# The masks of a diagonal block as the first products of their score banks, in a stick-breaking attention

## The reference, cut to what matters

```
def block(qb, qpb):
    z = jnp.einsum('bqhd,bkhd->bhqk', qb.astype(f32), kf) * (B_DH ** -0.5)
    valid = k_pos[None, :] < qpb[:, None]
    log_keep = jnp.where(valid, jax.nn.log_sigmoid(-z), 0.0)
    after = lax.cumsum(log_keep, axis=3, reverse=True) - log_keep
    a = jnp.where(valid, jnp.exp(jax.nn.log_sigmoid(z) + after), 0.0)
    return jnp.einsum('bhqk,bkhd->bqhd', a, vf)
```

## Time and profile before

| | us |
|---|---|
| three runs, median | 2052.14 (2051.48 to 2052.67) |
| the profiled execution, its own time | 2052.41 |
| its span in the trace | 2050.3 |
| TensorE busy in the span | 1908.9 |
| VectorE busy | 1126.9 |
| ScalarE busy | 1069.3 |

### The profile page before, as it was taken

How to read it: one execution, slowest core, us unless ns; L and a number is a source line. 1 busy time by engine, 2 the same in 40 slices (tenths; PEclk the granted TensorE clock), 3 DMA queues, 4 the chain that set the end, 5 groups by cost and what they waited for, 6 DMA issues and landing times. The chain is left out here.

```text
span 2050.3 us, 35228 instructions
## 1 busy us (share of the span) xinstructions
PE 1908.9 (93%) x11429; PEld 1634.9 (80%) x11429; DVE 1126.9 (55%) x2269; ACT 1069.3 (52%) x2556; POOL 387.1 (19%) x597
## 2 busy tenths in 40 slices
PE   4999999999999899986899999999999999989996
PEld 4888878878878699985777777777777777689995
DVE  5547456465564622554275757575657575754455
ACT  5455455454564521453375657575757575732335
POOL 0133132221331000453010101010101011100341
PEclk9999999999999999998999999999999999999999
DMA  4121121112211252212010101010101010233213
GB/s 152 57 63 36 46 60 56 50 47 57 62 36 47 96 141 66 64 65 73 21 58 27 57 26 57 26 57 26 57 26 57 26 57 26 96 111 97 62 44 131
DMA packets 161746, 124.18 MB, mean 61 GB/s; under 512 B 10992, under 2 KB 152624, under 8 KB 161648
## 3 DMA queue, kind: packets, MB, share of 16 engines
q1 hardware_dynamic: 160784, 122.85, 19.7%
q10 hardware_dynamic: 864, 0.20, 0.0%
HBM read 89.49 MB, written 33.52 MB: 60 GB/s over the span
## 5 line engine op out<-in xcount | busy, mean ns | idle before, releaser
L107 PE MATMUL pj<-area,h_high 128*128 128x384 f32 (+1 forms) x2304 | 666.6, 352 | 26.7 <-DVE lb_qk_low L1360 6.5
L107 PEld LDWEIGHTS pj<-area,h_high 128*128 128x128 f32 (+1 forms) x2304 | 413.6, 184 | 49.1 <-DVE lb_qk_low L1360 7.9
L107 PE MATMUL pj<-area,h_low 128*128 128x384 f32 (+1 forms) x1152 | 394.0, 342 | 0.0
L107 PEld LDWEIGHTS pj<-area,h_low 128*128 128x128 f32 (+1 forms) x1152 | 213.1, 185 | 8.7
L1532 POOL TENSOR_TENSOR lb_o<-lb_o,lb_keep 128x512 f32<-128x512 f32 (+3 forms) x80 | 77.1, 964 | 630.8 <-ACT lb_keep L1232 624.2
L1377 DVE SCALAR_TENSOR_TENSOR lb_s<-lb_sc,lb_m 128x512 f32<-128x512 f32 (+4 forms) x200 | 110.0, 550 | 85.1 <-ACT lb_m L1213 85.1
L1203 ACT ACTIVATE lb_m<-lb_sc 128x512 f32<-128x512 f32 (+4 forms) x200 | 89.1, 488 | 103.9 <-PE lb_sc L1614 41.5
L456 ACT ACTIVATE la_p<-la_sc,la_nm 128x128 f32<-128x128 f32 (+5 forms) x144 | 105.7, 737 | 33.7 <-DVE la_nm L653 32.8
L1408 DVE CAST lb_s_high<-lb_s 128x512 fp32r<-128x512 f32 (+1 forms) x192 | 109.0, 568 | 25.1
L1410 DVE TENSOR_TENSOR lb_s_low<-lb_s,lb_s_high 128x512 fp32r<-128x512 f32 (+1 forms) x192 | 114.6, 597 | 6.6
L651 DVE TENSOR_REDUCE la_mx<-la_sc 128x1 f32<-128x128 f32 (+5 forms) x144 | 107.6, 747 | 2.9
(11 more groups left out here) (307 smaller groups left out, 4470.1 us busy)
## 6 DMA issues: line engine op xcount, KB each, us to landing
stage<-in_a_w_in SPq DMA_DIRECT2D x60, 192.0 KB, 3.0
stage<-in_b_w_in SPq DMA_DIRECT2D x60, 192.0 KB, 2.6
stage<-in_ple_w_gate SPq DMA_DIRECT2D x22, 512.0 KB, 3.9
h_low<-o_t SPq DMA_DIRECT2D x14, 528.0 KB, 6.5
mix_b_xs<-x_mid SPq DMA_DIRECT2D x8, 528.0 KB
lift_xt<-in_x SPq DMA_DIRECT2D x8, 512.0 KB, 4.7
stage<-in_a_w_in SPq DMA_DIRECT2D x16, 256.0 KB, 5.2
out_ak<-la_tok SPq DMA_DIRECT2D x8, 512.0 KB, 3.3
```

What stands on the lines that cost most here:

```text
L107: last = pe.matmul(out, x, y, start=start and n == 0, stop=stop and n == 2, **kw)
```

## The change

On a diagonal pair the two masks no longer follow the score products; they come ahead of them and open the banks (`start=True`), and all score products of the pair add onto them (`start=False` for the first as well). They are a function of their own, `mask(i)`, which is called at the end of turn i - 1, behind the projection, and for pair 0 at the head of turn 0. It waits for the same count of `a` as `scores(i)`. The semaphore `z` is now raised by each head's third score product. The numbers of instructions, their shapes and the sample's pair stay as they are.

```
-                    q = span(c, b)[0]
+                    q, _, diagonal = span(c, b)
                     high, low = qk
                     for n, (x, y) in enumerate(((high, high), (low, high), (high, low))):
                         for s in units(i):
                             f = slice(UNITS[s][2] * DH, (UNITS[s][2] + 1) * DH)
                             last = pe.matmul(bank(s)[:, q:], x[f, 1, b * P:(b + 1) * P],
-                                             y[f, 0, c * QC + q:(c + 1) * QC], start=n == 0, stop=n == 2,
-                                             skip_group_check=True)
-                            if n == 2 and not span(c, b)[2]:
+                                             y[f, 0, c * QC + q:(c + 1) * QC], start=n == 0 and not diagonal,
+                                             stop=n == 2, skip_group_check=True)
+                            if n == 2:
                                 last.then_inc(S["z"], 1)
-                    if span(c, b)[2]:
-                        for s in units(i):
-                            pe.matmul(views(s)[0][:, 0:P], unit[:, :], hide[:, :], **masked).then_inc(S["z"], 1)
+
+                def mask(i):
+                    if not span(*PAIRS[i][0:2])[2] or PAIRS[i][0] == 2:
+                        return
+                    if i >= 2:
+                        pe.wait_ge(S["a"], at.nth("a", through(i - 2)))
+                    else:
+                        pe.wait_ge(S["a"], at.before("a"))
+                    for s in units(i):
+                        pe.matmul(views(s)[0][:, 0:P], unit[:, :], hide[:, :], start=True, stop=False,
+                                  skip_group_check=True)
...
                 for i in range(NP + 1):
+                    if i == 0:
+                        mask(0)
                     if i < NP:
                         scores(i)
...
+                    if i + 1 < NP:
+                        mask(i + 1)
                 values(NP - 1)
```

## The result

Five runs of the changed kernel took 2038.57 us in the median (2033.89 to 2045.80), five of the kernel before 2052.14; the ratio is 0.9938 with a 95% interval of 0.9917 to 0.9959, by which the change is worth 12.7 us. Run again on another chip it took 2040.48 against 2052.34, ratio 0.9937 (0.9925 to 0.9949). The executions also spread over 12 us, those of the kernel before over 2 us in the first runs and 5.5 to 9.4 in the later ones. The traced execution was the slowest of the first five, 2045.80 us with a span of 2043.7.

The account below looks back on a forecast made before the run. TensorE was taken to bound the kernel. Fewer tile-shape changes gave -5.25 us in looped groups, -0.15 in group 7 and +0.3 for turn 0, sum -5.1, clock 0: 2047.0 us, range 2043.2 to 2051.5.

Parts of the forecast that it names:

- What bounds the kernel: TensorE, busy 93% of the span; a saving on it in turns 2 to 13 shortens the group.
- Turn 0 and turn 1: Turn 0 loses 0.15 us, covered by turn 1's waits in groups 1 to 6; groups 0 and 7 charged 0.3; turn 1 nothing.
- Group 7: Turn 2 alone saves 0.15 us; turns 8 to 12 taken as 0, bounds -0.4 and +0.4; turn 0's loss charged.
- Sum without the clock: Whole kernel: -5.25 - 0.15 + 0.3 = -5.1 us, with the clock's effect taken as 0.
- turns 2 and 9 to 12: Masks behind the projection in its own shape save 0.15 us a turn, 5.25 us over seven looped groups.
- turn 3: Masks behind the 128*32 sample-row projection cost 0.26 + 0.37 us before and after, so nothing is saved.
- The clock: Half-clock stretches in groups 1 to 6 may move: bounds 7.8 us less to 4.7 more, taken as 0.
- B: Rival: masks behind the projection are held back as by another tile shape, nothing saved; 2052.1 to 2052.4 us, chance 0.06.
- C: Rival: first score pair of diagonal turns no longer runs side by side, so slower; 2053.1 to 2056.3 us, chance 0.04.
- A: Rival: moved half-clock stretches make all six groups like the longest three; 2051.7 us, half of that 2049.4; chance 0.18.
- D: Rival: fewer slow stretches, all six groups short; 2039.2 us, half of it 2043.1; chance 0.2.
- upper tail: Part of the forecast (clock within +-1.5 us of now, 0.52) counted as same, not faster; the line is 2048.0 us.

Follow-up runs that it names:

- The first filled pair: Nine unused products added in turn 1 of each looped group, to the kernel before (2040.11 us) and to the changed kernel (2028.68), on different chips.

## Why the prediction was off

**What bounds the kernel: right.** TensorE's order of work sets the group; releasing ScalarE 1.45 us later changes no turn of the looped groups.

**Turn 0 and turn 1: right, but for group 0.** It is 0.15 us more in turn 0, and the wait takes it; where the wait is filled, it shows (1.1 instead of 1.25 a group). The charge of 0.15 for group 0 was not due: no values stand ahead of its turn 0, the masks follow a projection product there, and the turn takes 6.25 us as before.

**Group 7: a little too small.** I took 0.15 less the charge for turn 0, that is nothing. Its turns 0 to 3 together take 28.4 us before and 28.1 after, 0.3 less. As a whole it took 88.1, 87.9, 89.4 and 86.4 us before and 87.2, 87.2, 87.2 and 86.2 after, 1.0 less in the mean, but with a spread as large, so the further 0.7 is not shown to be the order's.

**Sum without the clock.** It is 8.75 for the looped groups and 0.3 for the eighth: 9.0 us in place of 5.1, or 2043.1, just below the range. The first filled pair, in which nothing covers turn 0's loss, gives 8.4 for the order. So the terms for the turns were too small by 4 us, 2 of them in turns 2 and 9 to 12 and 1.8 in turn 3 (eight groups); against the 2047.0 forecast the medians missed by 6.5 to 8.4, and this is about half of it or more.

**The clock: left at 0.** I gave bounds and took no change. That the waits of turn 1 cost clock is shown by the filling: 11.8 us in the changed kernel, 12.6 and 12.1 in the kernel before. That the slow stretches decide some us, whatever the saving, is shown by the changed kernel itself: its second attention takes 788.91 us with 41.0 us at half clock and 794.20 with 54.6, at the same length of the turns at full clock. That the change won its further 3 us or so in this way is not shown: the traces have 51.2, 41.0, 47.8 and 54.6 us at half clock in the second attention after the change, and 51.2, 41.0, 47.8 and 44.4 before. By them nothing was won. And with the waits filled, where 3.4 to 13.7 us are left at half clock, the change is still worth 11.4 and 11.1 us in the medians, against 11.9 and 13.6 without the filling; that speaks against the waits of turn 1 as the main source. The cause of these 3 us stays open.

**The rivals.** B is refuted by 0.18 us from L107 to the mask, C by the first score pair, 0.50 us for two side by side as before (0.49). A did not come about: no execution of the change reached the 2047.0 that stood without it. D gives the measured time (2039.2), but not for its reason: the traces do not have fewer slow stretches, and the larger part of the gain is the order. That the time falls where D put it is luck.

**The chances.** They do not add up as stated. The forecast without its upper tail and D come to less than 0.52 + 0.2 = 0.72, not 0.74, and A, B and the tail to more than 0.24, not 0.23.

## What to carry to other kernels

Count the changes of the array's tile shape in TensorE's order as a cost of their own. Here taking two small products out from between two changes saved some 0.2 us, half of it the gap and half the weight load of the second product. Put a small full-shape product behind other full-shape products, where its loads run beside them; read from a trace which labels make a gap and which don't, each with its neighbour on both sides. Price a product by one of the same kind. Where a wait of a few microseconds makes the clock fall, compare turns at full clock, not groups or single executions; filling the wait with unused products took the spread of the changed kernel's executions from 9 us to 3.6 and made the gain easier to read.

## What the runs showed of the hardware that was not expected

Nine unused products of 512 columns in a wait of 2 us, 63 in all, made the kernel 11.8 us faster (2040.48 to 2028.68), since the stretches at half clock behind the wait went away; with six of them some came back (2033.86). A 128*128 product follows one of the shape 128*32 in 0.18 us, without a gap, while from two masks of 128 columns to the next load of the shape 128*64 or 64*128 it takes 0.37. And two products of 128 columns with the same stationary operand start 0.06 us apart behind a product of their own shape, but 0.16 apart behind a change of shape, as the second load is then not hidden.
